# Gate projections run as jobs inside the attentions, deep slots in the merge, and neighbourhood heads in pairs on the two halves of the array's rows

## The chip, the cores and the metric

One program runs on one core of a Trainium2 chip. The time is device microseconds of one execution, from start to end of the program. The engines are TensorE (PE in rows; PEld is its weight loads), VectorE (DVE), ScalarE (ACT), GpSimd (POOL) and SyncE (SP), which here only issues DMAs. TensorE runs at one of two clocks, 1.2 or 2.4 GHz; a granted clock of 1.00 in a row is 2.4 GHz, 0.50 is 1.2 GHz, and a value between them is a mixture of the two over time.

## The reference

Two layers over 256 context tokens and 512 latent tokens of width 1024. In each layer one normalised input `h` goes through one wide projection `w_in`, three token mixers read parts of it, and the merge gates them:

```python
z = concat([h_c, h_l]) @ w_in                      # parts: zl[0..14], zc[0..14]
oa = neighbourhood_attention(q, k, v, k_ctx, v_ctx, rpb)   # 4 heads of 64; 8 x 16 window + all context keys
ob = block_attention(...)                          # latent attention (MLA): 4 heads, 64 + 32 rotary, all keys
oc = gla_output(gla_bidirectional(...), zl[11])    # gated linear attention
y = (sigmoid(zl[12]) * (oa @ w_br_a)
     + sigmoid(zl[13]) * (ob @ w_br_b)
     + sigmoid(zl[14]) * (oc @ w_br_c)) @ w_out
x = x + mod[2] * y
x = x + mod[5] * expert_choice_moe(modulate(rms_norm(x)))   # 16 experts
```

Layer 0 does this for latent and context tokens, layer 1 for latent tokens alone (the context is then only keys). `zl[12..14]` are the gate projections: 1024 x 3072 weights of `w_in`, the largest part of it. All six modulation vectors of both layers come from `silu(c) @ ada_w + ada_b`.

## The kernel before

The kernel is written engine by engine: each engine has its own program, in the order in which it is to run, and they meet in semaphores (`wait_ge`, `then_inc`). So the order of the code of an engine is the order of its work, and whatever waits holds all that stands behind it on its engine.

Layer by layer the stages are: norm and projections (`project_job`, with TensorE taking three products for each pair of operand tiles: high part by high part, high by low and low by high, in the one-pass type fp32r; plain fp32 products are stored as two instructions each), the linear attention (`chunk_states`, `gla_outputs`) with more projections between its steps, the neighbourhood attention `attention(l, 0)` ("na" here), `latent_heads(l)` ("lat"), the latent attention `attention(l, 1)` ("mla"), `merge(l)` (gates, branches, output projection), then router and experts.

An attention is a list of units, one head and one tile of 128 queries each: 24 units in layer 0 (four heads by six tiles, two of them context tiles, which look at context keys only) and 16 in layer 1. In turn `u` of its loop TensorE does the scores of unit `u` into banks 0 to 3 (L1035 against 512 latent keys, L1036 against 256 context keys), in layer 0 eight products of a modulation half (L796, four column strips of the array side by side) that VectorE has to copy and TensorE has to sum (L781), the transposes of the probabilities of `u-1` (L1044 four latent tiles into bank 4, L1048 two context tiles into bank 5), then the values of `u-2` (L1061, up to 12 instructions, into bank 6). VectorE does the maxima of `u`, the copy of the context transposes (L1995) and the normalisation (L2002 to L2006), ScalarE the exponentials (L1539, L1540) and the copy of the latent transposes (L1549). The exponentials of `u` wait until unit `u-2` is normalised, because statistics have two slots. In layer 1 the six `dkv` projections stand between the units of na (`project_between`, L827). The 40 modulation halves of "na" and "mla" come from the weight ring in loads of 2 MB.

The merge runs over eight column tiles `j`, one or two token segments (512 latent, in layer 0 also 256 context) and three branches `b`. For each it does the gate projection, 8 by 3 products with `h` into an even bank, and the branch projection, 2, 2 or 4 by 3 products with `oT` into the odd bank beside it (both L1152). ScalarE takes the sigmoid of the gate bank (L1821), VectorE multiplies and adds (L2399 to L2402). The weights of a `j` (2 MB) lie in two ring slots and are split into high (ScalarE L1809) and low part (VectorE L2387) while `j-1` runs. After the last `j` the operands of the output projection are split (L1830, L2423), half 0 of them in one piece ahead of its first product (L1170); its halves are 512 columns each.

SP loads weights in one list, `ring_loads`; POOL loads small tensors, the bias and the latent weights.

## Time and profile before

| | us |
|---|---|
| median of 3 runs | 3082.44 |
| lowest, highest | 3052.95, 3086.1 |
| profiled execution, its own time | 3058.77 |
| its span in the profile | 3056.5 |

| layer, stretch | what TensorE's program does in it | length, us |
|---|---|---|
| 0, 342.2 to 623.8 | na, lat and mla, up to the merge's first product | 281.6 |
| 0, 623.8 to 975.0 | merge and output projection | 351.2 |
| 1, 1966.0 to 2222.1 | na (with the `dkv` projections), lat, mla | 256.1 |
| 1, 2222.1 to 2456.0 | merge and output projection | 233.9 |

How to read rows: a time is microseconds from the span's start; then the duration; the engine; the line of the kernel; the operation; what it writes and reads; rows x columns of the array that hold weights; and the shape of the moving operand. `x12` is a group of 12 neighbouring instructions, whose duration runs from the first start to the last end. A TensorE duration holds a modelled tail that overlaps the next instruction, so the cost of one in a stream is the distance between two starts. A bracket names the idle time ahead of it and what ended that. In windows the eighth value is the granted clock.

### The profile page before, as it was taken

The numbers are of one execution on the slowest core, as the hardware profiler recorded it, in microseconds if no ns is written. First come the engines' busy times: TensorE is split into PE (matmuls) and PEld (weight loads), VectorE is DVE, ScalarE is ACT, GpSimd is POOL, SyncE is SP. The second block draws the span as 40 slices with busy tenths as digits, with TensorE's granted clock in tenths as the row PEclk, the third lists the DMA queues.
The fourth block names the chain that finished last, engine by engine and source line by source line (L and its number), as shares of the span: only waits on it lengthen the run. The fifth ranks groups of instructions, "written<-read, shape, count | busy, mean of one in ns | idle before, by whom it ended". The sixth has DMA issues, their size and how long they took to land.

```text
span 3056.5 us, 42212 instructions
## 1 busy us (share of the span) xinstructions
PE 2717.5 (89%) x17806; PEld 1793.1 (59%) x17806; DVE 1012.9 (33%) x2091; ACT 686.0 (22%) x1306; POOL 33.4 (1%) x59
## 2 busy tenths in 40 slices
PE   5999998899988599999999689897799958999996
PEld 3888765688876535453444578775578743333332
DVE  4535344543233512312222544423343431111112
ACT  2511133322121211111111352123332221101101
POOL 1000000000000000000000000000000000000000
PEclk9999887989998599999999899956899979999998
DMA  5111552612222079786968111220023229999996
GB/s 187 49 42 37 167 197 83 194 28 69 70 97 84 28 294 351 293 350 260 382 258 349 58 58 45 56 55 1 1 62 104 83 110 361 390 399 379 410 384 240
DMA packets 233951, 539.78 MB, mean 177 GB/s; under 512 B 9734, under 2 KB 102128, under 8 KB 233776
## 3 DMA queue, kind: packets, MB, share of 16 engines
q1 hardware_dynamic: 231008, 531.34, 47.0%
q0 software_dynamic: 2768, 5.87, 0.9%
q8 instruction: 139, 2.28, 0.3%
q14 instruction: 36, 0.29, 0.0%
HBM read 532.91 MB, written 4.26 MB: 176 GB/s over the span
## 4 chain that ended last, share of the span: by engine, by line
PE 81%; DVE 8%; DMA 5%; ACT 4%; issue 2%; SPq 0%; DVEq 0%; POOL 0%; ACTq 0%
PE ps L1152 15%; PE ps L827 12%; PE ps L1219 11%; PE ps L1349 5%; PE ps L1061 4%; DMA arena<-in_moe_w_up 3%; PE ps L1170 3%; PE ps L1368 3%; PE ps L1391 2%; PE ps L1035 2%; PE ps L1412 2%; PE ps L1242 2%; PE ps L1246 2%; PE ps L1044 2%; PE ps L796 2%
## 5 line engine op out<-in xcount | busy, mean ns | idle before, releaser
L1219 PE MATMUL ps<-arena 128*32 128x512 f32 x2304 | 342.8, 604 | 5.8 <-issue 4.8
L1220 PE MATMUL ps<-arena 128*32 128x512 f32 x768 | 342.4, 604 | 0.0
L1349 PE MATMUL ps<-arena 128*64 128x512 f32 x1024 | 236.9, 609 | 34.6 <-DMA arena<-in_moe_w_up 31.3
L827 PE MATMUL ps<-m_lo,h_hi 128*128 128x256 f32 (+1 forms) x1248 | 243.5, 296 | 5.5 <-DVE m_lo L1882 3.9
L1219 PEld LDWEIGHTS ps<-arena 128*32 128x32 f32 x2304 | 94.1, 112 | 227.8 <-issue 225.2
L1152 PE MATMUL ps<-h_hi,m_hi 128*128 128x512 f32 (+1 forms) x576 | 205.6, 357 | 6.9 <-DVE m_lo L2387 6.9
L827 PEld LDWEIGHTS ps<-m_lo,h_hi 128*128 128x128 f32 x1248 | 201.5, 200 | 17.4 <-issue 12.8
L1152 PE MATMUL ps<-h_lo,m_hi 128*128 128x512 f32 (+1 forms) x576 | 205.2, 356 | 0.0
L1152 PE MATMUL ps<-h_hi,m_lo 128*128 128x512 f32 (+1 forms) x576 | 204.9, 356 | 0.0
L1349 PEld LDWEIGHTS ps<-arena 128*64 128x64 f32 x1024 | 74.5, 139 | 184.5 <-issue 180.8
L827 PE MATMUL ps<-m_lo,h_lo 128*128 128x256 f32 (+1 forms) x624 | 180.3, 289 | 0.0
L827 PE MATMUL ps<-h_hi,m_lo 128*128 128x512 f32 (+1 forms) x512 | 142.1, 354 | 9.5 <-DVE h_lo L1963 9.3
L1242 PE MATMUL ps<-arena 128*32 128x512 f32 x768 | 133.8, 597 | 2.9 <-issue 2.9
L1061 PE MATMUL ps<-arena 128*128 128x64 f32 x832 | 131.9, 320 | 3.4 <-DVE arena L2006 3.4
L1061 PEld LDWEIGHTS ps<-arena 128*128 128x128 f32 x832 | 129.8, 241 | 4.1 <-issue 4.1
L827 PEld LDWEIGHTS ps<-m_lo,h_lo 128*128 128x128 f32 x624 | 124.8, 200 | 0.0
L1368 PE MATMUL ps<-arena 128*64 128x512 f32 x512 | 119.6, 599 | 4.8 <-DMA arena<-in_moe_w_down 3.9
L1152 PEld LDWEIGHTS ps<-h_hi,m_hi 128*128 128x128 f32 x576 | 109.8, 191 | 23.2 <-issue 7.7
L1152 PEld LDWEIGHTS ps<-h_lo,m_hi 128*128 128x128 f32 x576 | 110.0, 191 | 15.3
L1152 PEld LDWEIGHTS ps<-h_hi,m_lo 128*128 128x128 f32 x576 | 109.7, 191 | 15.2
L1821 ACT ACTIVATE arena<-ps 128x512 f32<-128x512 f32 (+1 forms) x72 | 37.9, 527 | 326.9 <-PE ps L1152 326.9
L827 PEld LDWEIGHTS ps<-h_hi,m_lo 128*128 128x128 f32 x512 | 91.2, 190 | 28.7 <-issue 8.3
(358 smaller groups left out, 4548.0 us busy)
## 6 DMA issues: line engine op xcount, KB each, us to landing
arena<-in_moe_w_gate SPq DMA_DIRECT2D x128, 1024.0 KB, 7.9
arena<-in_moe_w_up SPq DMA_DIRECT2D x128, 1024.0 KB, 8.8
arena<-in_moe_w_down SPq DMA_DIRECT2D x128, 1024.0 KB, 8.3
ring<-in_ada_w SPq DMA_DIRECT2D x20, 2048.0 KB, 7.9
ring<-in_w_in SPq DMA_DIRECT2D x54, 512.0 KB, 5.1
ring<-in_w_in SPq DMA_DIRECT2D x18, 1024.0 KB, 5.1
ring<-in_w_out SPq DMA_DIRECT2D x4, 2048.0 KB, 8.6
arena<-in_ada_w SPq DMA_DIRECT2D x3, 2048.0 KB, 21.0
```

Of the source, the lines that this page charges most:

```text
L796: last = mm(ada_bank(h)[r:r + 2, 0:256], silc[:, :, k], w[:, k, 256 * (h % 2):256 * (h % 2) + 256], start=k < ADA_COLS, stop=k >= KD - ADA ...
L827: last = mm(to, stationary, moving, start=at == 0 and k == 0, stop=at == 2 and k == KD - 1)
L1035: mm(ps[2 * (u % 2)][:, :], q, kk[:, LAT], start=True, stop=True)
L1044: tr(ps[4][:, tile(t - CT)], prob[:, u % 2, tile(t)], ident)
L1061: last = mm(ps[6 + u % O_BANKS[l]][:, 0:64], probT[:, u % 2, kt, :], v, start=kt == 0, stop=kt == keys[-1])
L1152: last = mm(ps[2 * (q % 4) + bank][:, 0:size], w, x[:, k, seg], start=i == 0 and k == (0, kts[0])[bank], stop=i == 2 and k == (KD - 1, kts ...
L1170: last = mm(ps[2 + q % 4][:, :], y[:, k, tile(t)], w[:, k, :], start=i == 0 and k == 0, stop=i == 2 and k == KD - 1)
L1219: mm(ps[r][32 * b:32 * b + 32, :], c_xg[:, k, j, 32 * b:32 * b + 32], w, start=k == 0, stop=k == KD - 1)
L1220: last = mm(ps[r][96:128, :], c_xg[:, k, j, 32 * r:32 * r + 32], up[:, kk, 512:1024], start=k == 0, stop=k == KD - 1)
L1242: mm(ps[6][32 * b:32 * b + 32, :], rows[b], w[:, 0:512], **flags)
L1349: last = mm(bank[64 * c:64 * c + 64, :], p_xg[:, k, j, :], p_raw[(i + c) % PAIR_SLOTS][:, kk, 512 * half:512 * half + 512], start=k == 0, ...
L1368: last = mm(ps[5][64 * half:64 * half + 64, :], p_hidT[:, k, :], p_raw[i % PAIR_SLOTS][:, kk, 512 * half:512 * half + 512], start=k == 0, ...
```

## The change

1. **Gate projections as jobs.** The gate columns of `w_in` become 12 more chunks of 256 columns (`CHUNKS`, `MIX`) behind the 12 of the other projections, and run as jobs: 48 in layer 0 (24 with 512 moving columns, 24 with 256), 24 in layer 1 (512). `MIX_AT` says in which turn of na, lat and mla each half of a job stands; `mix_steps` issues a half, 12 products. VectorE copies the finished job out of its bank (`mix_taken`), POOL stores it to HBM (`mix_spill`). ScalarE and VectorE split the chunks between units (`mix_split`, `chunk_low`).
2. **Turn of an attention.** The order on TensorE is scores, modulation products, half a job, values of `u-2`, modulation sum, latent transposes of `u-1`, half a job, context transposes of `u-1`. The values go into the free columns of bank 5 (`ps[5][:, 256:320]`), since banks 6 and 7 are for jobs and modulation, so the context transposes of `u-1` wait until `u-2` is normalised. Statistics have four slots. `dkv` is done ahead of na again. Modulation halves load by 1 MB (`ada_load`), from na's and mla's own buffers.
3. **Pairs.** In na the units go pair by pair, so that two heads with the same query tile are neighbours; their keys lie on rows 0 to 63 and 64 to 127, and `paired_scores` issues both heads' products one behind the other, into different banks.
4. **Merge.** Only branch products are left in it. The gates come back from HBM in three slots (`mix_home`, one load per `j` of all three branches), the branch weights have four slots (`W_SLOTS`), the sigmoid is taken in place ahead of TensorE. The splits for the first half of the output projection stand between the `j` (`OUT_STEPS`); its first product takes `k` in the order `OUT_K`. The load of the second half of `w_out` is issued after the merge's last product is used.

```diff
+MIX = len(CHUNKS)
+CHUNKS += tuple([(O_M + b * D + 256 * i, 256)] for i in range(KD // 2) for b in range(3))
+        mix_out = [carve(ar, 10, SEQ), carve(ar, 54, SEQ)]
+        mix_home = [carve(x_flat, 0, 3, TOK), carve(hTf, 0, 3, TOK), carve(hTf, 9, 3, TOK)]
-        UNITS_AHEAD = {"na": 2, "mla": 0}
+        UNITS_AHEAD = 2
...
+        def mix_jobs(l):
+            return [(MIX + 3 * i + b, P * c, seg, 2 * i + c, b) for i in range(KD // 2) for b in range(3) for c in range(2) for seg in segments(l)]
+        MIX_AT = ([("na", u, place) for u in range(24) for place in (0, 1)] + [("lat", t, place) for t in range(NT) for place in (0, 1)]
+                  + [("mla", u, place) for u in range(18) for place in (0, 1)],
+                  [("na", u, place) for u in range(16) for place in ((0, 1) if u % 3 == 0 else (0,))]
+                  + [("lat", t, place) for t in range(1, NT - 1) for place in (0, 1)]
+                  + [("mla", u, place) for u in range(14) for place in ((0, 1) if u % 3 == 0 and u < 12 else (0,))])
...
+            def mix_steps(l, stage, u, place):
...
+                for k in range(KD // 2 * half, KD // 2 * (half + 1)):
+                    if k == 0:
+                        split_there(l, NJ[l] + i)
+                        first = i == 0 or MIX_AT[l][2 * i][0] != MIX_AT[l][2 * i - 1][0]
+                        if i > (0 if l == 0 or first else 1):
+                            pe.wait_ge(mix_copied, before("mix_copied", l) + (i if l == 0 or first else i - 1))
+                    for n, (w, h) in enumerate(((w_hi, h_hi), (w_hi, h_lo), (w_lo, h_hi))):
+                        last = mm(to, w[:, k, cols], h[:, k, seg], start=n == 0 and k == 0, stop=n == 2 and k == KD - 1)
...
+                def paired_scores(u):
+                    t = us[u][1]
+                    for e in range(2):
+                        if u + e >= 2:
+                            pe.wait_ge(s_exp, before("s_exp", idx) + u + e - 1)
...
+                def turn_context(u):
                     if u:
                         pe.wait_ge(p_dve, before("p_dve", idx) + u)
+                        pe.wait_ge(o_ok, before("o_ok", idx) + u)
...
                 for u in range(n + 2):
                     if u < n:
                         scores(u)
                     if l == 0:
-                        modulation_products(unit_events(("na", "mla")[i], u, "early"))
-                    if 1 <= u <= n:
-                        turn(u - 1)
-                    if i == 0:
-                        project_between(l, u)
+                        modulation_products(unit_events(stage, u, "early"))
+                    mix_steps(l, stage, u, 0)
                     if u >= 2:
                         values(u - 2)
                     if l == 0:
-                        modulation_products(unit_events(("na", "mla")[i], u, "last"))
+                        modulation_products(unit_events(stage, u, "last"))
+                    if 1 <= u <= n:
+                        turn_latent(u - 1)
+                    mix_steps(l, stage, u, 1)
+                    if 1 <= u <= n:
+                        turn_context(u - 1)
...
+            def mix_taken(l, stage, u):
...
+                dve.wait_ge(mix_up, before("mix_up", l) + i + 1)
+                if before("mix_up", l) + i >= 2:
+                    dve.wait_ge(mix_stored[i % 2], before("mix_stored", l) + 16 * (i // 2))
+                v.tensor_copy(mix_out[i % 2][:, 0:size], mix_bank(l, stage, i)[:, 0:size]).then_inc(mix_copied, 1)
+                if split_behind(l, NJ[l] + i) is not None:
+                    chunk_low(l, split_behind(l, NJ[l] + i))
```

On TensorE, in layer 0's na, a latent unit with its modulation half was this (L1035 and L1036 scores, L796 and L781 modulation, L1044 and L1048 transposes, L1061 values):

```order
L1035 MATMUL ps<-oT 128x512
L1036 MATMUL ps<-oT 128x256
L796 MATMUL ps<-ring,silc 2x256 x8
L1044 MATMUL ps<-cst,arena 128x128 x4
L1048 MATMUL ps<-cst,arena 128x128 x2
L1061 MATMUL ps<-arena 128x64 x6
L781 MATMUL ps<-cst,ada_row 128x2 x2
```

At the same place stands now the second half of a job (L917) between the latent transposes (L1130) and the context transposes (L1138), and behind these the scores of two heads (L1107, which every second turn has):

```order
L1130 MATMUL ps<-cst,arena 128x128 x4
L917 MATMUL ps<-h_hi,m_lo 128x256
L917 MATMUL ps<-h_lo,m_lo 128x256
L917 MATMUL ps<-h_hi,m_lo 128x256 x2
L917 MATMUL ps<-h_lo,m_lo 128x256
L917 MATMUL ps<-h_hi,m_lo 128x256 x2
L917 MATMUL ps<-h_lo,m_lo 128x256
L917 MATMUL ps<-h_hi,m_lo 128x256 x2
L917 MATMUL ps<-h_lo,m_lo 128x256
L917 MATMUL ps<-h_hi,m_lo 128x256
L1138 MATMUL ps<-cst,arena 128x128 x2
L1107 MATMUL ps<-oT 128x512 x2
```

What moved: the scores of two units are together, the job halves came in, and values and their modulation sum stand ahead of the transposes.

On VectorE in layer 0's na a unit was maxima (L1984 to L1989), the copy of the modulation row, the copy of the context transposes (L1995), normalisation:

```order
L1984 ISA arena,st<-ps,arena 128x512
L1984 ISA st 128x1
L1988 TENSOR_REDUCE st<-ps 128x1
L1989 TENSOR_REDUCE st<-st 128x1
L1924 COPY ada_row<-ps 98x256
L1995 COPY arena<-ps 128x256
L2005 RECIPROCAL st<-st 128x1
L2006 TENSOR_SCALAR arena<-ps,st 128x64
L1928 COPY modT<-ps 128x4
```

Now the copy of the job (L1997) and, in one unit of four, the split of a chunk (L1970) stand ahead of the copy of the context transposes (L2092), which is last:

```order
L2081 ISA arena,st<-ps,arena 128x512
L2081 ISA st 128x1
L2085 TENSOR_REDUCE st<-ps 128x1
L2086 TENSOR_REDUCE st<-st 128x1
L2021 COPY ada_row<-ps 98x256
L2102 RECIPROCAL st<-st 128x1
L2103 TENSOR_SCALAR arena<-ps,st 128x64
L2025 COPY modT<-ps 128x4
L1997 COPY arena<-ps 128x256
L1970 TENSOR_TENSOR m_lo<-ring,m_lo 128x2048
L2092 COPY arena<-ps 128x256
```

What moved: two operations that TensorE does not wait for at once stand ahead of one that its next values need.

On VectorE in layer 1's merge one `j` was three branches with wide splits of the next weights (L2387):

```order
L2399 TENSOR_TENSOR arena<-arena,ps 128x512
L2387 TENSOR_TENSOR m_lo<-ring,m_hi 128x1280
L2401 TENSOR_TENSOR arena<-arena,ps 128x512
L2402 TENSOR_TENSOR arena<-arena 128x512
L2387 TENSOR_TENSOR m_lo<-ring,m_hi 128x1280
L2401 TENSOR_TENSOR arena<-arena,ps 128x512
L2402 TENSOR_TENSOR arena<-arena 128x512
L2387 TENSOR_TENSOR m_lo<-ring,m_hi 128x1536
```

Now the splits (L2484) are those of the branch weights alone, and two splits for the output projection (L2491) follow from the fourth `j` on:

```order
L2505 TENSOR_TENSOR arena<-x_sb,ps 128x512
L2484 TENSOR_TENSOR m_lo<-ring,m_hi 128x256
L2507 TENSOR_TENSOR x_sb<-x_sb,ps 128x512
L2508 TENSOR_TENSOR arena<-arena,x_sb 128x512
L2484 TENSOR_TENSOR m_lo<-ring,m_hi 128x256
L2507 TENSOR_TENSOR x_sb<-x_sb,ps 128x512
L2508 TENSOR_TENSOR arena<-arena,x_sb 128x512
L2484 TENSOR_TENSOR m_lo<-ring,m_hi 128x512
L2491 TENSOR_TENSOR yT_lo<-arena,y_hi 128x512
L2491 TENSOR_TENSOR m_lo<-ring,m_hi 128x512
```

What moved: the gate weights' share went out of the three splits of a `j`, and two splits for the output projection came in from behind the merge.

## Rows read from the trace of the kernel before

**Rows 1.** Windows of the whole core, columns as in their first line.

```profile
core 0: us, PE busy (x) PEld busy (x) DVE busy (x) ACT busy (x) POOL busy (x), PEclk, DMA share, GB/s
342.20:623.80 281.60, 242.38 (x1761) 164.99 (x1759) 134.28 (x474) 86.80 (x253) 0.00 (x0) 0.86 0.48 165
466.00:504.20 38.20, 26.11 (x103) 16.61 (x103) 14.62 (x69) 12.41 (x32) 0.00 (x0) 0.77 0.00 0
623.80:975.00 351.20, 341.60 (x1832) 293.32 (x1832) 122.75 (x162) 74.29 (x106) 0.00 (x0) 0.99 0.20 57
1966.00:2222.10 256.10, 212.64 (x946) 160.73 (x946) 94.58 (x323) 75.15 (x214) 0.00 (x0) 0.70 0.07 17
2094.60:2127.40 32.80, 21.51 (x82) 13.07 (x83) 14.14 (x66) 9.93 (x26) 0.00 (x0) 0.76 0.00 1
2222.10:2456.00 233.90, 225.67 (x966) 182.71 (x966) 95.83 (x114) 61.12 (x80) 0.00 (x0) 0.99 0.28 82
2140.00:2190.00 50.00, 35.12 (x223) 26.39 (x222) 23.27 (x73) 18.69 (x55) 0.00 (x0) 1.00 0.00 1
```

**Rows 2.** Timeline of PE, layer 0, na: start, duration, what.

```profile
364.36 1.12 PE L1035 MATMUL ps<-oT 64*128 64x512 f32 x2
365.32 0.59 PE L1036 MATMUL ps<-oT 64*128 64x256 f32 x2
365.84 1.05 PE L796 MATMUL ps<-ring,silc 128*2 128x256 f32 x16
366.82 0.66 PE L1044 MATMUL ps<-cst,arena 128*128 128x128 f32 x4
367.31 0.38 PE L1048 MATMUL ps<-cst,arena 128*128 128x128 f32 x2
367.53 1.45 PE L1061 MATMUL ps<-arena 128*128 128x64 f32 x12
368.82 0.56 PE L781 MATMUL ps<-cst,ada_row 98*128 98x2 f32 x4
369.31 0.70 PE L1036 MATMUL ps<-oT 64*128 64x256 f32 x2
```

**Rows 3.** Timeline of PE, layer 1, na.

```profile
2005.88 0.63 PE L827 MATMUL ps<-m_lo,h_hi 128*128 128x160 f32 x2
...
2067.27 2.07 PE L1035 MATMUL ps<-oT 64*128 64x512 f32 x2
```

**Rows 4.** Timeline of PE in the merges, layer 0 and layer 1.

```profile
884.93 0.28 PE L1152 MATMUL ps<-h_lo,m_hi 128*128 128x256 f32 x1
885.05 0.28 PE L1152 MATMUL ps<-h_hi,m_lo 128*128 128x256 f32 x1
...
2222.14 0.76 PE L1152 MATMUL ps<-h_hi,m_hi 128*128 128x512 f32 x1 [3.44 <-DVE m_lo L2387]
...
2225.87 0.39 PE L1152 MATMUL ps<-h_hi,m_hi 128*128 128x512 f32 x1
2226.09 0.39 PE L1152 MATMUL ps<-h_lo,m_hi 128*128 128x512 f32 x1
```

**Rows 5.** Timeline of PE, end of layer 0's na: values behind a normalisation.

```profile
458.50 2.79 PE L1061 MATMUL ps<-arena 128*128 128x64 f32 x12 [0.86 <-DVE arena L2006]
```

**Rows 6.** The line that splits chunks (VectorE): min/median/max ns.

```profile
L1882 DVE TENSOR_TENSOR m_lo<-ring,m_lo x24: 1226/2282/2294, 44.4 to 1960.2; 128x2048 fp32r<-128x2048 f32 x20, 128x1024 fp32r<-128x1024 f32 x2, 128x1280 fp32r<-128x1280 f32 x2
```

**Rows 7.** Timeline of DVE at the end of layer 1's merge.

```profile
2398.81 0.69 DVE L2401 TENSOR_TENSOR arena<-arena,ps 128x512 f32<-128x512 f32 x1 [6.81 <-ACT arena L1821]
2399.53 0.69 DVE L2402 TENSOR_TENSOR arena<-arena 128x512 f32<-128x512 f32 x1
...
2401.59 0.69 DVE L2423 TENSOR_TENSOR m_lo<-ring,m_hi 128x512 fp32r<-128x512 f32 x1
2402.20 0.69 DVE L2423 TENSOR_TENSOR yT_lo<-arena,y_hi 128x512 fp32r<-128x512 f32 x1
```

**Rows 8.** DMA issues by line: KB each, median us to landing.

```profile
arena<-in_mla_w_ukv POOLq DMA_DIRECT2D x2, 256.0 KB, 8.6
```

More of the change, by code:

```diff
@@ L442, in hybrid_kernel @@
         ORDER = ("ga", "gqk", "gv", "og", "naqk", "nav", "dq", "dkv")
-        def between(l):
-            if l < DEPTH - 1:
-                return []
-            jobs = [("dkv", i) for i in range(len(projections(l)["dkv"]))]
-            return [(u, *job) for u, job in enumerate(jobs)]
         def first_job(l, name):
@@ L544, in moe_done, with slot_count @@
             return E // GE * 2 * NQ[l]
-        def ring_count(n):
-            return 16 * sum(6 if ring_loads[i][0] == "m" else 1 for i in range(n % 2, n + 1, 2))
+        def slot_count(l, j, slots):
+            return sum(1 for k in range(KD) if k % slots == j % slots) * l + j // slots + 1
         def tile(t):
@@ L557, in jobs_done, with units @@
             eng.wait_ge(proj_dve, before("proj_dve", l) + n // 2)
-        def units(l):
+        def units(l, i):
+            if i == 0:
+                return [(h, t) for pair in range(0, H, 2) for t in q_tiles(l) for h in (pair, pair + 1)]
             return [(h, t) for h in range(H) for t in q_tiles(l)]
@@ L682, in chunks_and_rows @@
                     chunk_load(l, 1)
-                for m in range(2, len(CHUNKS)):
+                for m in range(2, MIX + 2):
                     chunk_load(l, m)
-                sp.wait_ge(proj_up, before("proj_up", l + 1))
+                for stage in ("na", "lat", "mla"):
+                    for u in range(NT if stage == "lat" else UNITS[l]):
+                        if l == 0 and stage != "lat" and u < 2 * ADA[stage]:
+                            ada_load(stage, 2 * ada_first(stage) + u)
+                        i = mix_ended(l, stage, u)
+                        if i is not None and i + 1 < len(mix_jobs(l)) and mix_jobs(l)[i][0] != mix_jobs(l)[i + 1][0]:
+                            if mix_jobs(l)[i][0] + 2 < len(CHUNKS):
+                                chunk_load(l, mix_jobs(l)[i][0] + 2)
+                sp.wait_ge(mix_up, before("mix_up", l + 1))
             def pair_loads(l, g):
@@ L717, in _, with out_load @@
+            def out_load(l, half):
+                sp.dma_start(out_raw(half), a["w_out"][l][:, 512 * half:512 * half + 512].rearrange("(k p) n -> p k n", p=P)
+                             ).then_inc(out_in[half], 16)
+            for l in range(DEPTH):
+                chunks_and_rows(l)
+                for j in range(KD):
+                    merge_load(l, j)
+                sp.wait_ge(m_ok, before("m_ok", l) + 3 * NSEG[l] * (KD - 1))
                 if l == 0:
@@ L1526, in attention @@
                 idx = 2 * l + i
-                us = units(l)
+                us = units(l, i)
                 n = len(us)
@@ L1760, in _ @@
                 roots(NQ[l] - 1)
-                for name in ("dq",) if between(l) else ("dq", "dkv"):
+                for name in ("dq", "dkv"):
                     copies(l, name)
@@ L2322, in _ @@
                 turned(l, NQ[l] - 1)
-                for name in ("dq",) if between(l) else ("dq", "dkv"):
+                for name in ("dq", "dkv"):
                     copies(l, name)
```

363 lines of the change are left out of this document (194 added, 169 removed).

## Prediction

> **What bounds the kernel now.** I read the windows by stage first, then the timeline of TensorE inside one unit of an attention, then the timelines at the ends of the stages. In both merges TensorE is busy nearly all the time at 2.4 GHz, and it is what the others wait for: 351.2 us in layer 0 and 233.9 us in layer 1 [rows 1]. The attentions are the loose part: 281.6 us in layer 0 with a granted clock of 0.86, and 256.1 us in layer 1 with 0.70 [rows 1]. The reader should see two kinds of loss there. One is idle TensorE (212.6 of 256.1 us busy). The other is the clock: the same pair of score instructions takes 1.12 us in layer 0 and 2.07 us in layer 1 [rows 2, 3], so "busy" in layer 1 is largely work at 1.2 GHz. Products moved from the merges into the attentions cost the merge their full price and should cost the attention less, since they fill idle time and may bring the clock up.
>
> **Prices at 2.4 GHz.** In layer 0's na the distances between starts give a latent unit: scores 0.96 + 0.52, latent transposes 0.49, context transposes 0.22, values 1.29, together 3.48 us; a modulation half adds 0.98 + 0.49 = 1.47 [rows 2]. A context unit has only the 256-column scores, the context transposes and a third of the values: 0.52 + 0.22 + 0.43 = 1.17. A gate product is 0.12 us apart with 256 columns and 0.22 to 0.23 with 512 [rows 4], so a job of 24 is 2.88 or 5.45 us. Layer 0 has 24 of each, 199.9 us; layer 1 has 24 of the wide ones, 130.8 us.
>
> **The pairs.** No row shows row halves side by side. The nearest is L796: eight products of 256 columns on four column strips take 0.98 us, where one product of 256 columns on all columns takes 0.52 (L1036) [rows 2]; one after the other they would take about 4.2, so strips do run side by side. If row halves do as well, a latent pair saves 1.48 and a context pair 0.52: 8 x 1.48 + 4 x 0.52 = 13.9 us in layer 0, 8 x 1.48 = 11.8 in layer 1, 25.7 in all. The other bound is 0. Two instructions stand behind one another for each head, and they may keep each other in line, so I take the middle, 12.8 us (6.9 and 5.9). The Trainium skill (TensorEngine Tiling (Array Packing), Key Properties) says that a change of the tiling mode drains TensorE, and each pair stands between full-array products. It gives no price; no run here shows one. By the rule taken at its worst the pairs give 0 and the sum below is 12.8 us higher.
>
> **Attentions of layer 0.** Work at full clock: 32 latent units x 3.48 = 111.4, 16 context units x 1.17 = 18.7, 40 modulation halves x 1.47 = 58.8, jobs 199.9, together 388.8, less 6.9 for the pairs: 381.9. The lat stage takes 38.2 us at a clock of 0.77 with 26.1 busy [rows 1]. Its six jobs (counted above) stand between `up` and `turn` and hide part of its waits, say 5 us; 33.2 stay. Each attention ends with a drain: two waits behind a normalisation of 0.86 [rows 5], the last transposes with their copies, and six tiles through the array; about 6.5 us, 13 for both. I add 2 us for the first modulation load, which now waits for the first unit's maxima, 5 us for turns without a job at mla's end, and 2.4 for the first splits of the merge. Sum 437.5, against 281.6: **+156**.
>
> Are these turns bound by TensorE? A turn has 6 to 10 us of its work. Behind the second half of a job VectorE does the job's copy, in one of four turns the split of 2.28 us [rows 6], then the copy of the context transposes, before the values. TensorE has scores, modulation and the next half ahead of these values, 3 to 6 us; it is just enough. The maxima of the next unit are late by the same 3 us, and the transposes that need them stand a whole turn later. What TensorE waits for in vain I take as 0 here and price as a rival.
>
> **Attentions of layer 1.** 32 x 3.48 = 111.4, the `dkv` jobs 144 x 0.11 = 16 (an estimate in proportion to the 256-column products), jobs 130.8, less 5.9: 252.3. Lat: 32.8 [rows 1] less 4. Drains 11 for both. A turn with only its first half of a job has just the latent transposes (0.49) between the values and the wait for their normalisation (0.86) [rows 5], 0.4 us lost in each of 20 turns, 8. Turns without a job, start and first splits 6. Sum 306, against 256.1: **+50**.
>
> This takes the clock as 1.00. Layer 1's na is at the low clock at 2005.88, where a pair of narrow `dkv` products takes 0.63 us, and still at 2067.27 [rows 3]: the `dkv` products in it did not bring the clock up for good. For it speak layer 0's na, where units with a modulation half run at the full pace [rows 2], mla, which holds 1.00 with 35.1 of 50 us busy [rows 1], and above all the merge: it begins at the low clock (0.76 us) and is at 0.22 us a product 3.7 us later [rows 4]. Half a job at the low clock is 12 x 0.43 = 5.1 us of just such products. So each half should bring the clock up, and the question is only whether the rest of a turn lets it fall again.
>
> **Merges.** Layer 0: branch products 8 x (24 x 0.227 + 24 x 0.12) = 66.6 us. VectorE per `j`: linked operations of 512 columns are 0.72 apart, unlinked 0.60 [rows 7]. Latent segment 3.4, context 2.0, weight splits 1.2, output splits 0.9 + 0.6: 8.1, so 65 and a start of 8.4 for the first splits. VectorE is now the bound by a little, 73 with TensorE's last piece; then output products 12 x 5.45 = 65.4, gate rows 5.4, handovers 3: 147. Before, 351.2: **-204**. Layer 1: TensorE 43.6; VectorE 3.4 + 1.2 + 0.6 + 0.6 = 5.8 a `j`, with its start 51; output 43.6 + 5, handovers and small waits 5: 105 against 233.9: **-129**. The gates come back by DMA, 1.2 MB a `j` with three slots, asked for two `j` ahead (12 to 17 us). A POOL load of 256 KB lands in 8.6 us [rows 8].
>
> **The stores.** `mix_taken` waits for the store of the job before last. Jobs are 6 to 9 us apart, so a store has 12 to 17 us; at 8.6 [rows 8] it is hidden. Without that cover VectorE waits, and behind it stand the context copy and all maxima.
>
> **Sum.** +156 + 50 - 204 - 129 = -127. Against the profiled execution's own 3058.8: 2932. That execution lies 23.7 us below the median of the three (3052.95 to 3086.1), so I add half of that gap: **2944 us**.
>
> **Rivals.**
>
> - *The sum holds* (0.62). Its own range: pairs -13 or +13, median gap -12 or +12, small waits up to 25: 2905 to 2985.
> - *Waits in the turns* (0.18). The in-order chain on VectorE and ScalarE (maxima, job copy, split, context copy) comes late by 0.5 to 1 us in each of the 80 turns that hold units: 40 to 80 us more, 2985 to 3025. For it speaks that the cover is just enough; against it that VectorE is busy 134 of 281.6 us [rows 1] and gets only 48 copies and 12 splits, about 55 us.
> - *The clock stays low in layer 1's na* (0.12). Its units and jobs, about 56 + 60 us at full clock less the pairs, double in part or whole: 30 to 110 us more, 2975 to 3055.
> - *Slower than before* (0.04): the clock stays at 1.2 GHz through both attentions of layer 1. About 240 us of work is doubled: 2944 + 240 = 3184. It decides once more than 127 us of that work, about half, runs at the low clock. Only the low stretch of na speaks for it; the merge's recovery speaks against it.
> - *The stores or the gate loads do not keep up* (0.04): from 17 us a store VectorE stands; at 25 us it is 4 us in each of 72 jobs, 4 x 72 = 288 more and 3232; at 20 us 1.5 x 72 = 108 more and 3052. The measured 8.6 us speaks against it.
>
> About 1% is what a measurement of this kernel can tell from no change. Faster by more than that needs under 3052 (or 3028 by the own time): 0.62 + 0.18 and nearly all of 0.12, together 0.91. Within 1%: 0.04. Slower: 0.05. The range reaches from the lower end of the first case into the waits and the low clock: 2905 to 3010.
>
> **What would show each step.** Attentions with granted clock over 0.9 in both layers, about 437 and 306 us long; merges with output of 147 and 105 us; in the merges VectorE nearly without gaps. The pairs: four score instructions of 512 columns within 1.0 to 1.5 us instead of 1.92. Right is also that no copy of a job waits for a store. The prediction is wrong if L917's neighbours show idle TensorE behind VectorE of over 0.5 us a turn, if na in layer 1 has a clock near 0.5, or if the merge's `j` takes over 10 us.

## The result, and the profile of the changed kernel

The changed kernel takes 2931.8 us (median of four, 2929.9 to 2934.0) against 3076.2 for the kernel before (3053.0 to 3086.1): a ratio of 0.954, 95% interval 0.948 to 0.960. The prediction was 2944, range 2905 to 3010. The profiled execution took 2929.9 us, against 3058.8 before, 128.9 less.

| us, from the profiled executions | before | forecast | changed |
|---|---|---|---|
| attentions, layer 0 | 280.8 | 437.5 | 433.1 |
| attentions, layer 1 (with `dkv`) | 255.9 | 306 | 297.6 + 16.1 of `dkv` ahead of them |
| merge and output, layer 0 | 352.7 | 147 | 145.4 |
| merge and output, layer 1 | 232.7 | 105 | 97.7 |
| own time | 3058.8 | 2932 | 2929.9 |

Stages are counted from the first score to the first branch product, and from there to the first gate row behind the output products. Windows of the changed kernel, columns as in [rows 1]: both attentions, merge with output, for layer 0 and then layer 1.

```profile
344.90:778.00 433.10, 411.70 (x2910) 320.95 (x2910) 179.62 (x533) 109.12 (x265) 26.04 (x48) 0.98 0.50 164
778.00:923.40 145.40, 139.71 (x680) 116.34 (x680) 94.09 (x163) 51.48 (x105) 0.00 (x0) 0.98 0.27 92
1929.20:2226.80 297.60, 263.19 (x1379) 206.25 (x1379) 130.79 (x355) 95.98 (x223) 13.04 (x24) 0.95 0.25 80
2226.80:2324.50 97.70, 92.59 (x388) 73.66 (x388) 67.83 (x113) 40.03 (x79) 0.00 (x0) 0.98 0.34 112
```

The granted clock is 0.98 and 0.95 in the attentions, where it was 0.86 and 0.70 [rows 1]. The stages lie close to the forecast. But the experiments below show two parts of the change that each take most of the time away alone, and the prediction priced only one of them.

Timeline of PE of the changed kernel, layer 0's na: start, duration, what.

```profile
368.58 0.38 PE L1138 MATMUL ps<-cst,arena 128*128 128x128 f32 x2
368.90 1.13 PE L1107 MATMUL ps<-oT 64*128 64x512 f32 x4
369.86 0.60 PE L1109 MATMUL ps<-oT 64*128 64x256 f32 x4
370.39 0.83 PE L859 MATMUL ps<-arena,silc 128*2 128x256 f32 x12
```

Four score instructions of 512 columns take 0.96 us from start to start, what two took [rows 2]; four of 256 take 0.53. The halves of the rows run fully side by side.

What TensorE waited for in layer 1's attentions of the changed kernel: in total, times, longest.

```profile
PE ps L1138 <- DVE arena L2103: 8.8, 21, 0.4
PE ps L1149 <- DVE arena L2092: 7.0, 9, 3.2
PE ps L1187 <- DVE arena L2451: 6.1, 1, 6.1
PE ps L1207 <- DVE arena L2466: 3.8, 1, 3.8
```

The 8.8 us are context transposes behind a normalisation, in turns with one half of a job or with none. The 7.0 us are values behind the copy of the context transposes, worst where the low split of a chunk (2.28 us) stands ahead of it on VectorE. The stores of the jobs, in the list of DMA issues, KB each and median us to landing:

```profile
mix_spill<-arena POOLq DMA_DIRECT2D x48, 256.0 KB, 2.8
```

### The profile page after: what moved, and what is told of

It is laid out like the page before. It is cut to its first block, busy times and chain, and to the rows that moved or that the text cites. A ratio compares the mean times of both kernels' runs of the same rounds, so it can differ in the third digit from the quotient of the medians.

```text
span 2928.2 us, 42639 instructions
## 1 busy us (share of the span) xinstructions
PE 2626.2 (90%) x17806; PEld 1726.6 (59%) x17806; DVE 1042.5 (36%) x2187; ACT 689.8 (24%) x1330; POOL 73.1 (2%) x131
## 3 DMA queue, kind: packets, MB, share of 16 engines
q8 instruction: 139, 2.28, 0.3%
## 4 chain that ended last, share of the span: by engine, by line
PE 82%; DVE 8%; DMA 5%; ACT 3%; issue 2%; SPq 0%; DVEq 0%; POOL 0%; ACTq 0%
PE ps L890 12%; PE ps L1305 11%; PE ps L917 11%; PE ps L1435 6%; PE ps L1256 4%; PE ps L1239 4%; PE ps L1149 3%; DMA arena<-in_moe_w_up 3%; PE ps L1454 3%; PE ps L1477 2%; PE ps L1498 2%; PE ps L1328 2%; PE ps L1332 2%; PE ps L859 2%; PE ps L1388 1%
## 5 line engine op out<-in xcount | busy, mean ns | idle before, releaser
L917 PE MATMUL ps<-h_hi,m_lo 128*128 128x512 f32 (+1 forms) x1152 | 345.9, 371 | 1.7 <-DVE arena L1997 1.7
L917 PEld LDWEIGHTS ps<-h_hi,m_lo 128*128 128x128 f32 x1152 | 207.8, 190 | 53.6 <-issue 16.8
L890 PEld LDWEIGHTS ps<-m_lo,h_hi 128*128 128x128 f32 x1248 | 198.0, 196 | 17.1 <-issue 12.5
L917 PE MATMUL ps<-h_lo,m_lo 128*128 128x512 f32 (+1 forms) x576 | 204.9, 356 | 0.0
L890 PE MATMUL ps<-h_hi,m_lo 128*128 128x512 f32 (+1 forms) x512 | 144.3, 358 | 9.5 <-DVE h_lo L2060 9.2
L917 PEld LDWEIGHTS ps<-h_lo,m_lo 128*128 128x128 f32 x576 | 109.6, 190 | 15.5 <-issue 2.2
L1970 DVE TENSOR_TENSOR m_lo<-ring,m_lo 128x2048 fp32r<-128x2048 f32 (+2 forms) x48 | 106.0, 2208 | 28.1 <-ACT m_lo L1562 28.1
L1149 PEld LDWEIGHTS ps<-arena 128*128 128x128 f32 x832 | 105.0, 195 | 18.5 <-issue 10.1
L1149 PE MATMUL ps<-arena 128*128 128x64 f32 x832 | 105.4, 275 | 9.6 <-DVE arena L2092 9.6
L890 PEld LDWEIGHTS ps<-h_hi,m_lo 128*128 128x128 f32 x512 | 92.8, 193 | 29.1 <-issue 8.2
L1997 DVE COPY arena<-ps 128x512 f32<-128x512 f32 x72 | 43.3, 601 | 166.5 <-PE ps L917 166.5
L2145 DVE TENSOR_TENSOR arena<-arena,ps 96x512 f32<-96x512 f32 x16 | 10.9, 682 | 254.0 <-ACT arena L1654 254.0
```

The lines of the kernel that those rows point to most:

```text
L890: last = mm(to, stationary, moving, start=at == 0 and k == 0, stop=at == 2 and k == KD - 1)
L917: last = mm(to, w[:, k, cols], h[:, k, seg], start=n == 0 and k == 0, stop=n == 2 and k == KD - 1)
L1149: last = mm(ps[5][:, 256:320], probT[:, u % 2, kt, :], v, start=kt == 0, stop=kt == keys[-1])
L1970: v.tensor_tensor(lo, raw, hi.bitcast(F32), ALU.subtract).then_inc(p_lo_ok, 1)
```

## The experiments

Each kernel was timed in four executions; the median stands first, the profiled one's own time behind it. Those of `before` lay between 3051 and 3091 us, those of any changed kernel with one exception within 9 us of each other, so differences of stages are taken from the profiled executions.

### Which part took the time away

**Pairs alone, in the kernel before.** Units in pairs, paired scores, and what they need: four slots of statistics.

```diff
+                return [(h, t) for pair in range(0, H, 2) for t in q_tiles(l) for h in (pair, pair + 1)]
+                        if u % 2 == 0:
+                            paired_scores(u)
-                        act.wait_ge(o_ok, before("o_ok", idx) + u - 1)
-                    c = 32 + 8 * (u % 2)
+                    if u >= 4:
+                        act.wait_ge(o_ok, before("o_ok", idx) + u - 3)
+                    c = 32 + 8 * (u % 4)
```

> The kernel before with the pairs alone: its units in pairs of heads, the paired scores and the four slots of statistics that they need; no jobs, the old merge. Theory A (what the pairs save on TensorE shows in the time): layer 0's na 14 us shorter; in layer 1's na 12 us at full clock and up to 24 at the low one; profiled execution 3022 to 3033 against 3059. Theory B (without the jobs TensorE isn't the bound there: it was busy 212.6 of 256.1 us in layer 1, and the units wait for maxima, exponentials and copies): 0 to 8 us, 3050 to 3059, and idle TensorE takes the place of the shorter scores; the jobs are what makes the pairs worth something.

Measured: 2951.6 us (2951.4), 107 below the profiled kernel before. Both theories were far off: layer 1's attentions fell from 255.9 to 177.1 us, layer 0's from 280.8 to 252.3. No price of the pairs reaches that, so the slots that came with them were tried by themselves.

**The slots of statistics alone, in the kernel before.** Only the last five lines of that diff.

> The kernel before with the four slots of statistics alone (an exponential waits for the normalisation four units back and not two); no pairs, no jobs, the old order of a turn. Pairs and slots together took 79 us from layer 1's attentions (255.9 to 177.1) and 29 from layer 0's. Theory A (the slots are the larger part: in the kernel before every exponential waits for the normalisation at the end of the turn, then the transposes wait for it, 24.1 us in 16 times in layer 1, and in these gaps the clock falls): layer 1's attentions 190 to 200 us, layer 0's 260 to 268, the whole 2970 to 2985. Theory B (the pairs are the larger part, twice their worth at 1.2 GHz): layer 1's attentions 220 or more, the whole 3015 or more.

Measured: 2961.9 us (2959.7), 99.1 less than before, with layer 1's attentions at 177.0 and layer 0's at 259.5. Theory A holds and was too small. (One of its four executions took 3019 us at a mean granted clock of 0.925, the others 2959 to 2964 at 0.938 to 0.944; no trace of that one is kept.) A turn of layer 1's mla in the kernel before, already at full clock:

```profile
2142.29 1.45 PE L1061 MATMUL ps<-arena 128*128 128x64 f32 x12
2143.58 1.08 PE L1035 MATMUL ps<-arena 96*128 96x512 f32 x2
...
2144.17 0.28 DVE L2006 TENSOR_SCALAR arena<-ps,st 128x64 f32<-128x64 f32 x1
...
2144.57 0.69 ACT L1539 ACTIVATE arena<-ps,st 128x512 f32<-128x512 f32 x1 [3.11 <-DVE arena L2006]
...
2146.44 0.63 PE L1044 MATMUL ps<-cst,arena 128*128 128x128 f32 x4 [1.35 <-ACT arena L1549]
...
2148.41 1.08 PE L1035 MATMUL ps<-arena 96*128 96x512 f32 x2
```

It goes round: values, normalisation (L2006), exponential (L1539, held until then) with ScalarE's copy behind it, transposes, values; 4.83 us a turn, of which TensorE stands 1.35. The same with four slots:

```profile
2069.97 0.69 ACT L1540 ACTIVATE arena<-ps,st 128x512 f32<-128x512 f32 x1 [1.58 <-DVE st L1990]
...
2070.50 1.08 PE L1035 MATMUL ps<-arena 96*128 96x512 f32 x2
...
2071.10 0.28 DVE L2007 TENSOR_SCALAR arena<-ps,st 128x64 f32<-128x64 f32 x1
...
2071.85 0.62 PE L1044 MATMUL ps<-cst,arena 128*128 128x128 f32 x4
...
2073.81 1.08 PE L1035 MATMUL ps<-arena 96*128 96x512 f32 x2
```

The exponential now starts behind the maxima (L1990) and ahead of the normalisation; a turn takes 3.31 us and TensorE does not wait. The Trainium skill (Perfetto Trace Analysis, Optimization Strategy) says that the same gap repeating on the engine that should be saturated can mean too few buffers; the trace agrees, with the same 1.35 us in turn after turn. That is mla. In layer 1's na the larger part is the clock. Windows from na's first score to the first products of lat's first turn, before and with four slots:

```profile
1966.20:2108.80 142.60, 128.11 (x526) 99.62 (x527) 47.02 (x169) 36.88 (x111) 0.00 (x0) 0.60 0.12 30
```
```profile
1942.40:2034.20 91.80, 81.08 (x526) 64.16 (x527) 45.93 (x169) 37.19 (x111) 0.00 (x0) 0.94 0.19 47
```

The same 526 recorded products keep TensorE busy 128.1 us at a granted clock of 0.60 and 81.1 us at 0.94: 47 of the 50.8 us. In the kernel before the clock falls in the middle of na. Windows up to the fall and behind it:

```profile
1966.20:1993.40 27.20, 24.00 (x165) 19.46 (x165) 12.82 (x35) 6.91 (x21) 0.00 (x0) 1.00 0.01 2
1993.40:2076.20 82.80, 82.80 (x285) 63.57 (x284) 23.49 (x85) 18.97 (x56) 0.00 (x0) 0.50 0.21 51
```

Ahead of the fall TensorE stood three times for ScalarE: 0.72 us, and twice 1.24 us, which ended at 1985.2 and 1992.8. Behind it the records show no gap for 83 us, and the clock stayed low all the same. The kernel with four slots has only the first of these waits there (0.65 us) and keeps 1.00 until 2021.0. That the slots brought the clock back is shown by this run; that these two short waits made it fall is not, because in mla TensorE stood 1.35 us in every turn at a clock of 1.00 [rows 1].

**Scores one by one, in the changed kernel.** Each unit's scores in its own turn.

```diff
-                        if u % 2 == 0:
-                            paired_scores(u)
-                        return
+                        r = 64 * (h % 2)
+                        q, kk = naqT[r:r + 64, h // 2, tile(t)], nakT[r:r + 64, h // 2, :]
...
```

> The changed kernel with the neighbourhood scores of each unit issued alone in its own turn, in the same order of units; everything else stays. Theory A (the two row halves run fully side by side, and the turns are bound by TensorE): four score instructions of 512 columns take 0.96 us in pairs, as two do alone, so 1.48 us more for each latent pair and 0.52 for each context pair: layer 0 attentions 433 to 447 us, layer 1 298 to 309, the whole 25.7 us more, near 2958. Theory B (what the pair saves is lost again in the odd turn, which has no scores and waits for VectorE): 10 us or less, 2932 to 2942, with fewer waits of the values for the context copy than the 7.0 us of layer 1 now.

Measured: 2950.2 us (2951.3): 18.4 more by the medians, 21.3 by the profiled ones; layer 0's attentions 445.6 and layer 1's 307.2, that is 12.5 and 9.6 more. Each layer lies in the range that A gave it, the whole between A and B. The forecast's middle of 12.8 was too low. In the kernel with slots and without jobs the pairs are worth less: 8.3 us (2959.7 to 2951.4), 7.2 in layer 0 and nothing in layer 1, where na kept TensorE busy 74.4 us and not 81.1, but at a clock of 0.89 and not 0.94.

**Two slots of statistics, in the changed kernel.**

```diff
-                    if u >= 4:
-                        act.wait_ge(o_ok, before("o_ok", idx) + u - 3)
-                    c = 32 + 8 * (u % 4)
+                        act.wait_ge(o_ok, before("o_ok", idx) + u - 1)
+                    c = 32 + 8 * (u % 2)
...
```

> The changed kernel with two slots of statistics as before; pairs, jobs, the new order of a turn and the deep slots stay. Theory A (with a job's half between them and the values ahead of the transposes, an exponential's wait for the normalisation two units back is covered): under 5 us more, 2932 to 2937; jobs and new order on one side and the slots on the other heal the same wait. Theory B (the slots are what lets the turns run at TensorE's pace also with jobs): the transposes wait 1 to 2 us in each of some 80 turns, 2990 to 3060.

Measured: 2950.6 us (2946.0), 18.8 more by the medians, 16.1 by the profiled ones: between the two. This run has all of the change but the slots, and it is 112.7 us faster than the kernel before (3058.8 to 2946.0). Layer 0 shows what A says (436.7 us against 433.1, and the same code of layer 0 ran in 433.1 to 436.8 in the other kernels); layer 1 went from 297.6 to 314.0. Its window, and the waits in it:

```profile
1931.70:2245.70 314.00, 269.56 (x1379) 210.54 (x1379) 131.28 (x355) 93.89 (x223) 13.04 (x24) 0.93 0.24 78
```

```profile
PE ps L1149 <- DVE arena L2091: 12.6, 8, 3.8
PE ps L1138 <- DVE arena L2102: 8.3, 20, 0.4
PE ps L1107 <- ACT arena L1623: 6.4, 5, 2.5
```

These waits are 9 us longer than in the changed kernel (7.0, 8.8 and 2.5 there). The granted clock is 0.93, where it is 0.70 in the kernel before with the same two slots: jobs and new order bring the clock up too. They cover the old wait in layer 0, where every turn of a unit holds a whole job, and less well in layer 1, where most do not; that this is the reason was not tried. Slots on one side, jobs and order on the other heal the same wait: the slots are worth 99 us without jobs and 16 with them.

**The sum of parts**, by profiled own times: slots -99.1, pairs on top -8.3, and jobs, new order and new merge on top of both -21.5 (2951.4 to 2929.9). In that last step the attentions grew by 180.8 us in layer 0 and by 136.6 in layer 1 (`dkv` counted), 317.4 for jobs priced at 330.7, and the merges with output shrank by 343. The order of adding decides what each part seems worth: all but the slots first is -112.7, the slots on top -16.1. Whether the jobs or the new order of a turn do the larger part of the 112.7 was not tried.

### What the jobs' places are worth

**No job in layer 1's na, and none in most of its mla.** Two kernels that change one table each, layer 1's places. Na bare:

```diff
-                  [("na", u, place) for u in range(16) for place in ((0, 1) if u % 3 == 0 else (0,))]
-                  + [("lat", t, place) for t in range(1, NT - 1) for place in (0, 1)]
-                  + [("mla", u, place) for u in range(14) for place in ((0, 1) if u % 3 == 0 and u < 12 else (0,))])
+                  [("lat", t, place) for t in range(NT) for place in (0, 1)]
+                  + [("mla", u, place) for u in range(18) for place in (0, 1)])
```

Mla bare but for its first four turns, in place of the same lines:

```diff
+                  [("na", u, place) for u in range(16) for place in (0, 1)]
+                  + [("lat", t, place) for t in range(1, NT - 1) for place in (0, 1)]
+                  + [("mla", u, place) for u in range(4) for place in (0, 1)])
```

> The changed kernel with layer 1's jobs taken out of its na: six in the lat stage (both halves of every turn), eighteen in mla (both halves of every turn). Theory A (the jobs hold the clock up in na): na without them is at 1.2 GHz for most of its length, granted clock 0.5 to 0.7, a latent pair's scores near 3.0 us; na takes about 90 to 100 us for its 16 units although 60 us of jobs have left, mla about 162; the attentions of layer 1 take 305 to 320 us and not 298, the whole 2940 to 2955. Theory B (the clock doesn't hang on the jobs): granted clock over 0.9 in na, about 72 us; the whole 2910 to 2930, since mla's waits behind single halves (8.8 us) go too.

> The changed kernel with layer 1's jobs packed early: both halves in each of na's 16 turns, the lat stage as now, and only four jobs in mla, whose last 12 turns of units are bare. Theory A (a bare turn costs 3.85 us as now, and no turn with a whole job waits for a normalisation): na 23 us longer, mla 28 us shorter, the attentions of layer 1 about 293 and not 298 us, the whole near 2927; the clock stays at 1.0 in bare mla, as in the kernel before (35 of 50 us busy). Theory B (spreading the jobs over all turns is what pays, because bare turns leave TensorE idle or bring the low clock): bare turns 5 to 7 us, the whole 2945 to 2975.

Measured: na bare 2923.6 us (2925.2), mla bare 2918.6 (2920.4). Both are faster than the changed kernel, by 8 and 13 us. Layer 1's na without a job (the window ends with the first half of lat's first job), and its mla where only the first four turns hold one:

```profile
1930.00:2021.80 91.80, 67.34 (x406) 49.05 (x407) 45.80 (x167) 38.08 (x109) 0.00 (x0) 0.87 0.04 12
```
```profile
2127.00:2218.70 91.70, 81.68 (x457) 63.97 (x457) 42.80 (x124) 32.58 (x87) 2.17 (x4) 0.95 0.25 84
```

The clock was 0.87 in the window of bare na: not the 0.5 to 0.7 that my theory A gave it, and less than B's 0.9. Most of what is missing lies at the end: 0.95 from 1930.0 to 1995.0, and 0.68 from there on, where TensorE waits 6.1 us for mla's normalisation. With four slots the jobs are not needed to hold the clock up; na holds most of it bare, with or without the `dkv` products (0.94 above). For mla bare, theory A's working came out: from na's start to lat 19.8 us more (158.1 against 138.3), from there to the merge 29.3 less (130.0 against 159.3). A turn with a single half or none waits 0.4 us for the normalisation (9 times in the changed kernel's na, once in mla bare's, where every turn holds a whole job). Whole jobs have a price of their own: 4.7 us in nine waits behind the context copy.

**Two slots for the merge's weights and for the gates.** `W_SLOTS, MIX_SLOTS = 2, 2` in place of 4, 3.

> The changed kernel with two slots for the merge's branch weights (not four) and two for the gates (not three). Theory A (the deep slots are what hides the loads): the weights of the next column block are asked for when the block before the current one is done and land 5.3 to 6.1 us later, but their split is due 2 us into the block, so each of six or seven blocks stands about 4 us: 24 to 28 us more in each layer, the whole 2980 to 2990. Theory B (two slots do, since a block takes 8.8 us in layer 0 and 5.9 in layer 1, about as long as a load): under 8 us more, 2932 to 2940.

Measured: 2951.4 us (2953.8), 19.6 more by the medians: 4.1 in layer 0's merge and 18.1 in layer 1's. ScalarE and TensorE in layer 1's merge:

```profile
ACT m_hi L1892 <- DMA ring<-in_w_br_c: 23.6, 6, 5.5
```
```profile
PE ps L1239 <- DVE m_lo L2484: 13.5, 16, 4.4
```

In layer 1 the mechanism is A's: ScalarE stood about 4 us for the weights of each of six blocks. TensorE had part of that covered, and its merge grew by 18.1 us, not by 24 to 28. In layer 0, whose blocks take 8.9 us, the load is nearly hidden. The deep slots are worth their place where a block (6.1 us in layer 1) is as short as a load (6.1 us in the changed kernel's list). Weights and gates were cut together; the waits name the weights, with one of 1.5 us for the gates.

**Splits for the output projection behind the merge.** All of `OUT_STEPS` after the last `j`.

> The changed kernel with the splits for the output projection all behind the merge's last block and not spread over its blocks. Theory A (VectorE has room for them in layer 0's blocks but is itself the bound in layer 1's): behind the merge a pair of splits takes 1.6 us of VectorE in layer 0 and 1.4 in layer 1, against 0.68 us of products, so TensorE stands about 7 us in each; layer 1's blocks get 1.2 us shorter each and give that back; the whole 6 to 10 us more, 2938 to 2942. Theory B (the blocks are bound by TensorE in both layers): nothing is given back, 14 to 18 us more, 2946 to 2950.

Measured: 2941.3 us (2945.1), 9.5 more by the medians. Merge and output together took 7.8 us more in layer 0 and 5.2 in layer 1. At the end of layer 1's merge TensorE stands ahead of the output products:

```profile
PE ps L1257 <- DVE yT_lo L2492: 5.9, 1, 5.9
```

A holds by the medians; the two stages' 13.0 us lie between A and B. The blocks of layer 1 gave back 1.0 us in all (first to last branch product 46.9 us, then 45.9), since behind the first only three of them were longer than the 5.4 us that TensorE needs. Those of layer 0 gave back nothing (69.6 both times).

**One buffer for the jobs' results.** The copy of a job waits for the store of the job just before.

```diff
-        mix_out = [carve(ar, 10, SEQ), carve(ar, 54, SEQ)]
+        mix_out = [carve(ar, 10, SEQ), carve(ar, 10, SEQ)]
...
-                if before("mix_up", l) + i >= 2:
-                    dve.wait_ge(mix_stored[i % 2], before("mix_stored", l) + 16 * (i // 2))
+                if i:
+                    dve.wait_ge(mix_stored[(i - 1) % 2], before("mix_stored", l) + 16 * ((i + 1) // 2))
```

> The changed kernel with one buffer for the jobs' results and not two, so that the copy of a job waits for the store of the job just before it. Theory A (a store lands 2.8 us after its issue, about 3.4 us after the copy, and copies are at least 5 us apart): no copy waits, 2930 to 2936. Theory B (the 8.6 us of my row of a load on the same queue): a copy would wait up to 3 us where jobs are 6 to 9 us apart, and VectorE's context copy and maxima behind it: 60 to 150 us more, 2990 to 3080.

Measured: 2934.6 us (2932.4), 2.7 more by the medians. Of 72 copies three waited:

```profile
DVE arena L1997 <- DMA mix_spill<-arena: 8.4, 3, 6.1
```

A store needs no second buffer here, but for the few that land late (up to 7.3 us in layer 1).

**A pair's scores head by head.** Lower rows 512 and 256 columns, then upper rows.

```diff
-                    if t >= CT:
-                        for e, (q, kk) in enumerate(operands):
+                    for e, (q, kk) in enumerate(operands):
+                        if t >= CT:
                             mm(ps[2 * e][:, :], q, kk[:, LAT], start=True, stop=True)
-                    for e, (q, kk) in enumerate(operands):
                         mm(ps[2 * e + 1][:, 0:CTX], q, kk[:, CX], start=True, stop=True).then_inc(s_up, 1)
```

> The changed kernel with a pair's scores issued head by head: 512 and 256 columns of the lower rows, then 512 and 256 of the upper rows. Theory A (two products overlap when they follow one another and lie on different row halves): only the 256 columns of the first head run beside the 512 of the second; a latent pair takes about 2.4 us and not 1.49, a context pair as now; 16 x 0.95 = 15 us more, near 2947. Theory B (TensorE finds the free half whatever the order): no change, 2932. Theory C (the overlap needs equal shapes side by side): a latent pair is serial, 2.97 us, 16 x 1.48 = 24 us more, 2956.

Measured: 2931.1 us (2930.3), no change: theory B. Its timeline has 1.50 us from the first score to what follows, the changed kernel 1.49 (368.90 to 370.39):

```profile
368.55 1.14 PE L1107 MATMUL ps<-oT 64*128 64x512 f32 x4
369.51 0.60 PE L1108 MATMUL ps<-oT 64*128 64x256 f32 x4
370.05 1.05 PE L859 MATMUL ps<-arena,silc 128*2 128x256 f32 x16
```

### A faster version

**Own bank for the outputs, split behind the copy, on top of mla bare.** In layer 1 the outputs lie in bank 7 and no longer beside the context transposes, and the wait of these for the normalisation is gone. The lines that matter:

```diff
+            return ps[7][:, 0:64] if l else ps[5][:, 256:320]
...
                     if 1 <= u <= n:
                         copy(u - 1)
+                    mix_low(l, ("na", "mla")[i], u)
```

> The changed kernel with layer 1's jobs packed as in e5_mla_bare (2918.6) and two waits taken away: in layer 1 the outputs have a bank of their own (the jobs of a unit stage share one, as in layer 0), so the context transposes wait for no normalisation; and a chunk's low split stands behind the copy of the context transposes, not ahead of it. Theory A (a wait of TensorE there is time on the path): the 5.8 us (L1138) and most of the 5.9 us (L1149) of e5's layer 1 go, and 1 to 2 in layer 0: about 10 us less, 2906 to 2911. Theory B (the waits move: the first half of a job waits for the copy of the job before, or maxima come late behind the split): within 3 us of 2918.6.

Measured: 2913.7 us (2919.0), 5 less by the medians than mla bare (1.4 by the profiled ones), where A gave 10 and B at most 3. Layer 1's attentions fell from 288.1 to 280.8. The waits of L1138 and most of those for the context copy went, but half of them came back as B says, at the first product of a job behind the copy of the job before (L921):

```profile
PE ps L1194 <- DVE arena L2464: 6.3, 1, 6.3
PE ps L921 <- DVE arena L2004: 4.7, 8, 0.8
```

**The gaps at na's end filled.** Jobs also in na's two last turns, and a whole one behind its last transposes; mla has fewer. The call that issues the latter:

```diff
+                for place in (0, 1):
+                    mix_steps(l, "end", 0, place)
                 pe.wait_ge(mla_n, before("mla_n", l) + NT)
```

> g1_own_bank with jobs in the gaps at the end of na: both halves in its two last turns and one whole job behind its last transposes, where TensorE waits 6.1 to 6.6 us for the mla normalisations; they leave the turns of mla, of which layer 1 keeps one with a job. Theory A (a job there costs nothing): 1.8 + 5.4 us less in each layer, 2892 to 2898. Theory B (mla is left bare in layer 1 and falls to the low clock, 16 units of 3.5 us that double in part): what the gaps give is lost, 2905 to 2930, with a granted clock under 0.9 in layer 1's mla.

Measured: 2896.7 us (2896.0), 17.0 less than the step before and 35 less than the changed kernel; against the kernel before, 0.948 (0.946 to 0.950) in its own comparison. Layer 0's attentions fell by 10.9 us (436.2 to 425.3) and layer 1's by 6.6 (280.8 to 274.2). Theory A. Layer 1's mla:

```profile
2124.60:2193.10 68.50, 62.36 (x385) 48.96 (x385) 38.60 (x120) 30.63 (x86) 0.54 (x1) 0.95 0.30 100
```

Mla with one job in its turns keeps a clock of 0.95; B did not come.

## Why the prediction was right, and where it was not

- **The time and its stages.** Right: attentions +156 and +50 against +152 and +58 (with the `dkv` products, which ran ahead of them), merges -204 and -129 against -207 and -135, sum -127 against -129. The half of the gap between own time and median that I added (12) was not there: the changed kernel's executions lie about 4 us apart.
- **What gives the gain.** Half right. The prediction opens with moved products that "fill idle time and may bring the clock up", and with two slots of statistics they do, together with pairs, order and merge: 112.7 us less, and a granted clock of 0.93 in layer 1's attentions where it was 0.70. What failed is a term put at nothing without a reason. I added up each turn as TensorE's work, which silently took the exponential's wait as gone, and never priced the edit that takes it away, though the description of the kernel before names that wait. The slots of statistics alone take 99.1 us away; on top of all the rest they take 16.1. With the slots in place the jobs cost the attentions 317.4 of their 330.7 us: they fill 13 us of idle time and not the 125 (330.7 less 156 and 50) of my sum. The working summed a state, not a change, and so could not say which edit earned it.
- **The clock taken as 1.00 in layer 1.** It was 0.95. The reason given, that half a job brings the clock up, fits the run with two slots (na at 0.94 with jobs, 0.60 in the kernel before). It is not the only way: with four slots and no job na had 0.87 and 0.94, mla nearly bare 0.95.
- **The pairs.** "I take the middle, 12.8": they were worth 18.4 to 21.3, between the middle and the upper bound of 25.7; the row halves run fully side by side, and the rest of the 25.7 does not reach the time. The Trainium skill (TensorEngine Tiling (Array Packing), Key Properties) says that a change of mode drains TensorE. A pair stands between products on all rows, and starts 0.32 us behind the first of two transposes (368.58 to 368.90), where values follow such a pair of transposes in 0.22 [rows 2]: so no drain of more than about 0.1 us shows ahead of a pair, and the unpaired scores lay on 64 rows too. The rival that gave the pairs 0 did not come.
- **Layer 1's attentions.** With pairs at their full worth my sum would have been 300; 313.7 came. The wait behind single halves was right (8.8 us against 8), the missing part is the 7.0 us behind the context copy, of which my working took 0 and named the risk, the 2.5 us of scores behind an exponential, and the clock.
- **The stores.** "At 8.6 it is hidden": hidden it was, but the nearest row was a load. Stores of the same 256 KB landed in 2.8 us (median); one buffer would nearly do.
- **Waits in the turns, the rival with 0.18.** Wrong by its size: 18 us of such waits in layer 1, 6 in layer 0, not 40 to 80. The stay at the low clock did not come.
- **Merge.** Right in both layers: 8.9 and 6.1 us a block (70.9 and 48.9 for eight) against 8.1 and 5.8, and the sum of both stages right. In layer 0 the bound is TensorE by a little and not VectorE: without the output splits its blocks were no shorter. The working's own terms said so, 66.6 us of products against 65 of VectorE; the start of 8.4 made VectorE look longer.

## What to carry to other kernels

Look for a wait that goes round: the result of a unit gates the next exponential, and in mla the same gap of 1.35 us stood in every turn. Two more slots of a few statistics broke it. In layer 1's na the higher clock that came with them was worth more than the waits themselves, 47 of 50.8 us.

Price a change edit by edit, against the kernel without it and against the kernel with all the rest. Here two parts of the change healed the same wait: the slots take 99.1 us alone, all the rest 112.7, both together 128.9. A sum of the new state's work can give the right time and say nothing of which edit earned it. And once the wait was gone, moving the gate projections was worth little (21.5 us with order and merge), while the gaps at the stages' ends took jobs nearly for nothing (17.0 us).

## What was not expected of the hardware

- The two halves of the array's rows work off their products independently of the order of issue: issued 512, 256, 512, 256, a pair's scores took 1.50 us against 1.49, and the records show all four of the 512 columns ahead of the 256. The Trainium skill (TensorEngine Tiling (Array Packing), Key Properties) says that tiles operate independently; the trace agrees.
- The same products had a granted clock of 0.60 in one kernel and 0.94 in the other, with TensorE busy about nine tenths of the time in both (128.1 of 142.6 us, 81.1 of 91.8). At 1.2 GHz the records showed TensorE without a gap for 83 us and the clock did not rise, so a busy share close to 1 can hide a low clock. Short waits stood on both sides: two of 1.24 us ahead of the fall in na, and one of 1.35 us in every turn of mla, where the clock stayed at 1.00. The runs do not say which waits cost the clock.
- A 256 KB store issued by POOL lands in 2.8 us (median of 48, none over 7.3); the two 256 KB loads of [rows 8] took 8.6.
